# Expert passes of a decoder step: a ring of eleven up slabs, and TensorE's up products written out

## The chip, the cores and the metric

The kernel runs on one core of a Trainium2 chip. The metric is the device time of one execution in microseconds (us). TensorE is called PE here, VectorE DVE, ScalarE ACT and SyncE SP, as in the profile. SP issues nearly all transfers (DMAs); PE's own instructions are fetched by the DMA engines too, and the profile counts them as "instruction" packets.

## The reference

Two layers of a decoder trunk on 288 tokens (256 of a prompt, 8 x 4 of samples), model width 1024. Each layer has a token mixer (three recurrent branches, gates, an output projection) and a feed-forward part. In layer 0 that is dense, in layer 1 it is a mixture of eight experts, two for each token. All is fp32.

```python
def moe_swiglu(h, router, w1, w3, w2):          # w1, w3: 8 x 1024 x 2816, w2: 8 x 2816 x 1024
    logits = (h @ router).astype(jnp.float32)
    top_v, top_i = lax.top_k(logits, TOP_K)
    probs = jax.nn.softmax(top_v, axis=-1)
    gate = jnp.sum(jax.nn.one_hot(top_i, N_EXPERTS) * probs[..., None], axis=-2)
    out = jnp.zeros(h.shape, jnp.float32)
    for e in range(N_EXPERTS):
        out = out + gate[..., e:e + 1] * ((silu(h @ w1[e]) * (h @ w3[e])) @ w2[e])
    return out
```

## The kernel before

The whole step is one program. The change bears on its last part, `experts`, and on one place of `mix_out` just before it.

**Passes.** Each expert is one pass over its own tokens, gathered into at most 91, 88, 73, 85, 76, 82, 79 and 70 columns in the eight passes (`CAPS`). Seven passes are written out one behind the other for PE and SP (`FIXED`), each with its own width; the eighth stands in a loop that runs `rest` times (once in the profiled execution) to take in an overflow.

**Slabs.** Weights come in slabs of 128 partitions x 8 blocks x 128 columns, 512 KB. A pass has 44 up slabs (22 pairs of w1 and w3, `UP_SLABS`) and 24 down slabs (`DOWN_SLABS`; 8 of them hold 384 KB). Up slabs go through `ring`, eight places that the rest of the program uses too; slab n lies in place n % 8. Down slabs go through six places in the dead tensor `proj` (`DRING`). Each landing adds 16 to the place's semaphore (`slab_in`, `down_in`), each slab that PE has finished adds 1 to `slab_done`, and a load waits on that count.

**SP's order in a pass** (L2519 to L2541), all in one queue, each load waiting for its own place: down slabs 0 to 5 of this pass; up slabs 8 to 43; the number of the following expert; that expert's up slabs 4 to 7 and 0 to 3 (`FREED`); down slabs 6 to 23. The last pass loads eight up slabs of a following expert, too, which nobody reads.

**PE's order in a pass** (`expert`, L2681): the up products, 44 slabs, as a loop of five turns over eight slabs (`Fori`, body of 8 calls of `up`) and then four slabs behind the loop, 12 slabs of code. A slab is 16 matmuls, K block by K block, each in two halves of 64 output rows (`narrow_products`, L454). The trace has two matmul records and two weight loads for each of them, so 32 and 32 a slab. Then the scatter matrix (L2648), the gathering of the next pass's tokens (L2619, L2626), and a loop of four turns over the 24 down slabs (L2661), the scatter of the results into `xT` (L2672) and transposes (L2679).

Products of pair f go to the PSUM banks 2f % 4 and 2f % 4 + 1; ACT takes silu of the first (L2744), DVE multiplies (L2958), and counts `w1_free` and `w3_free` hold PE back until a bank is free. Inside the loop the values waited for are worked out from its turn in registers.

**Before the experts.** In `mix_out` of layer 1, SP loads the second group of the gate and branch slabs (`load_group`), the eight slabs of the output projection (`load_first_group`), and then up slabs 0 to 7 of expert 1. The tensors `y_ret` and `lora_w` hold sums of activations and weights for the first three pairs of slabs of the join and nothing after that.

Of the kernel before, what the change touches and what calls it, by code (L numbers as in the profile page):

```python
# [20 lines left out]
ACT = mybir.ActivationFunctionType  # L21

D = 1024
# [64 lines left out]


UP_SLABS = 2 * FT  # L90
DOWN_SLABS = 24
HALF = T // 2
PAIRS_UP, PAIRS_DOWN = KT // 2, FT // 2
# [127 lines left out]
def build(nc, xT_in, w_mix, w_lora, w_rank, w_gkup, vec_in, vecf_in, router_in, w_ff, s_ret, s_gla, s_rw,  # L221
# [130 lines left out]
            self.end = w.at  # L352

    slab_in = [nc.alloc_semaphore(name=f"slab_in{s}") for s in range(RING)]
    slab_done = nc.alloc_semaphore(name="slab_done")
    rank_in = [nc.alloc_semaphore(name=f"rank_in{s}") for s in range(2)]
    wr = lora_w[:, :, :].rearrange("p k n -> p (k n)")[:, 0:512].rearrange("p (s n) -> p s n", s=2)
# [77 lines left out]
    def slab_arrived(pe, p, g, s):  # L435
        pe.wait_ge(slab_in[s], (g + (fills_before(layer, s) + fills(p, s) + 1)) * 16)

    def load_ff_slab(sp, e, j, s, done, n=KT):

        sp.wait_ge(slab_done, done)  # L440
        sp.dma_start(ring[:, s, 0:n], w_ff[e, j, :, 0:n]).then_inc(slab_in[s], 16)
# [5 lines left out]
            mm = nc.tensor.matmul(out, ring[:, s, k, :], x, start=(k0 + k == 0), stop=(k0 + k == last - 1))  # L447
        mm.then_inc(slab_done, 1)

    def narrow_products(pe, s, out, rhs, n=KT, k0=0, last=KT):  # L450

        for k in range(n):
            for c in range(2):
                mm = nc.tensor.matmul(out[64 * c:64 * c + 64], ring[:, s, k, 64 * c:64 * c + 64], rhs[:, k0 + k, :],  # L454
                                      start=(k0 + k == 0), stop=(k0 + k == last - 1))
        mm.then_inc(slab_done, 1)

    FIRST, MIDDLE, LAST_TWO = bank[0:6:3], bank[1:6:3], bank[2:6:3]
# [1665 lines left out]
    def mix_out(nc, block, sig, layer, delta, joined):  # L2124
# [31 lines left out]
        @block.sync  # L2156
        def _(sp):
            load_group(sp, S_RW_OUT, 1)
            load_first_group(sp, S_OUT)
            if dense:  # L2160
                for j in range(FF_SLABS):
                    load_ff_slab(sp, 0, j, j % RING, FF0 + j - RING + 1, dense_slab_width(j))
                    if j == UP_SLABS:
                        sp.wait_ge(sig("normed"), KT)
                        sp.dma_start(vec[:, :], vec_in[layer + 1]).then_inc(sig("next_vec"), 16)
                        sp.dma_start(lora_w[:, :, :], w_lora[layer + 1]).then_inc(sig("next_low"), 16)
                        sp.dma_start(gkup[:, :], w_gkup[layer + 1]).then_inc(sig("next_up"), 16)
                load_next_layer(sp)
                sp.wait_ge(sig("next_up"), 16)
            else:  # L2170
                for j in range(RING):
                    load_ff_slab(sp, 1, j, j, FF0 + j - RING + 1)
# [287 lines left out]
    def experts(nc, block, sig, layer, merge, rs):  # L2460
# [26 lines left out]
        down_in = [sig(f"down_in{s}") for s in range(DRING)]  # L2487
        LG, LT, RANK = bank[6], bank[1], bank[0][:, 0:4 * NE]
        HG, SC, DOWN, SUM = bank[4:8], bank[1], bank[2:4], bank[0]
        OTOK, ADD = (bank[6], bank[4]), (bank[7], bank[5])  # L2490
        FF0 = slabs_before(layer, len(STREAM))
        FREED = 4, 5, 6, 7, 0, 1, 2, 3
        TILES = ((0, 128), (128, 128), (256, 32))

        def passes(eng):
# [3 lines left out]
        def count(p, per, k):  # L2499

            i, done = p
            return i * per + (done * per + k)
# [5 lines left out]
        @block.sync  # L2508
        def _(sp):
            def freed_up(p, n):  # L2510

                if n >= RING:
                    return count(p, FF_SLABS, FF0 + n - RING + 1)
                return count(p, FF_SLABS, FF0 - FF_SLABS + max(range(n, UP_SLABS, RING)) + 1)

            def load_up(p, e, n):
                load_ff_slab(sp, e, n, n % RING, freed_up(p, n))

            def load_down(p, e, d):  # L2519
                if d >= DRING:  # L2520
                    sp.wait_ge(slab_done, count(p, FF_SLABS, FF0 + UP_SLABS + d - DRING + 1))
                else:
                    sp.wait_ge(slab_done, count(p, FF_SLABS, FF0 - DRING + d + 1))
                n = slab_width(UP_SLABS + d)
                sp.dma_start(down_ring[:, d % DRING, 0:n], w_ff[e, UP_SLABS + d, :, 0:n]).then_inc(down_in[d % DRING], 16)

            e = 1
            for q in range(FIXED):
                p = 0, q
                for d in range(DRING):  # L2530
                    load_down(p, e, d)
                for n in range(RING, UP_SLABS):
                    load_up(p, e, n)
                if q == 0:
                    sp.wait_ge(sig("ctl"), 1)
                following = sp.value_load(ctl[0:1, q:q + 1], min_val=1, max_val=NE)
                for n in FREED:
                    load_up((0, q + 1), following, n)
                for d in range(DRING, DOWN_SLABS):
                    load_down(p, e, d)  # L2540
                e = following  # L2541
            rest = passes(sp)
            with sp.Fori(0, rest) as i:
                e = sp.value_load(ctl[0:1, bass.ds(i + (FIXED - 1), 1)], min_val=1, max_val=NE)
                following = sp.value_load(ctl[0:1, bass.ds(i + FIXED, 1)], min_val=1, max_val=NE)
                p = i, FIXED
                for d in range(DRING):
                    load_down(p, e, d)
                for n in range(RING, UP_SLABS):
                    load_up(p, e, n)  # L2550
                for n in FREED:
                    sp.wait_ge(slab_done, freed_up((i, FIXED + 1), n))
                    settle(sp)
                    sp.dma_start(ring[:, n], w_ff[following, n]).then_inc(slab_in[n], 16)
                for d in range(DRING, DOWN_SLABS):
                    load_down(p, e, d)
            for k in range(0, KT, 2):
                sp.wait_ge(sig("normed"), k + 2)
                sp.dma_start(yT_out[:, k:k + 2, :], hT[:, k:k + 2, :]).then_inc(sig("stored"), 16)
            sp.wait_ge(sig("stored"), 4 * 16)  # L2560
            for s in range(RING):
                per = len(range(s, UP_SLABS, RING))
                fill = fills_before(layer, s) + fills(len(STREAM), s) + FIXED * per + 1
                sp.wait_ge(slab_in[s], rest * (per * 16) + fill * 16)
                settle(sp)

        @block.tensor
        def _(pe):
# [44 lines left out]
            def gather_tokens(n, cap):  # L2613

                pe.wait_ge(sig("picked"), n)
                for j in range(2):
                    for r in range(4):
                        rows = slice(NS * r, NS * r + NS)
                        mm(HG[r][:, CAP * j:CAP * j + cap], htok2[rows, j, :], gather[rows, 2, 0:cap], start=(j == 0),  # L2619
                           stop=False)  # L2620
                for r in range(4):
                    for j in range(2):
                        k = 4 * j + r
                        for i in range(2):
# [3 lines left out]
                                          start=False, stop=(j == 1 and i == 1))  # L2628
                    last.then_inc(sig("hg_ps"), 1)

            def up(p, cap, n, turn):

                i, done = p
                s = n % RING
                per = len(range(s, UP_SLABS, RING))
                fill = fills_before(layer, s) + fills(len(STREAM), s) + done * per + n // RING + 1
                pe.wait_ge(slab_in[s], turn * 16 + (i * (per * 16) + fill * 16))
                pe.wait_ge(sig("w3_free" if n % 2 else "w1_free"), turn * (RING // 2) + count(p, FT, n // 2 + 1))
                if n in (2, 3):
                    pe.wait_ge(sig("oT"), count(p, KT, n - 1))  # L2640
                narrow_products(pe, s, bank[n % 4][:, 0:cap], hg[:, :, 0:cap])

            def scatter_matrix(p):

# [36 lines left out]
            def expert(p, cap, next_cap):  # L2681

                pe.wait_ge(sig("hg"), count(p, 1, 1))
                settle(pe)
                with pe.Fori(0, UP_SLABS // RING) as g:
                    for n in range(RING):
                        up(p, cap, n, g)
                for n in range(UP_SLABS // RING * RING, UP_SLABS):
                    up(p, cap, n, 0)
                scatter_matrix(p)  # L2690
                pe.wait_ge(sig("otok"), count(p, KT, 2))
                pe.wait_ge(sig("added"), count(p, KT, 2))
                gather_tokens(count(p, 1, 2), next_cap)
                pe.wait_ge(sig("w3_free"), count(p, FT, FT + 2))
                settle(pe)
                with pe.Fori(0, KT // 2) as t:
                    for m in range(2):
# [38 lines left out]
        def _(act):  # L2736
            ac, cp = nc.scalar.activation, ACT.Copy

            def silu(p, f):
                act.wait_ge(slab_done, count(p, FF_SLABS, FF0 + 2 * f + 1))  # L2740
                if f == 0:
                    settle(act)
                act.wait_ge(sig("w3_free"), count(p, FT, f + 1))
                ac(act1[:, f % 2, :], bank[2 * f % 4][:, 0:CAP], ACT.Silu).then_inc(sig("w1_free"), 1)  # L2744

            def take_down(p, m):
                act.wait_ge(slab_done, count(p, FF_SLABS, FF0 + UP_SLABS + 3 * m + 3))
# [58 lines left out]
        def _(dve):  # L2806
# [144 lines left out]
            def expert(p):  # L2951

                for f in range(FT):
                    dve.wait_ge(slab_done, count(p, FF_SLABS, FF0 + 2 * f + 2))
                    if f == 0:
                        settle(dve)
                    dve.wait_ge(sig("w1_free"), count(p, FT, f + 3))
                    tt(hid[:, f, :], bank[(2 * f + 1) % 4][:, 0:CAP], act1[:, f % 2, :],  # L2958
                       ALU.mult).then_inc(sig("w3_free"), 1)
                    choose(p, f)  # L2960
                take_gathered(count(p, 4, 4))
# [348 lines left out]
```

## Time and profile before

| | us |
|---|---|
| median of 3 runs | 2516.02 |
| lowest and highest run | 2513.42, 2517.08 |
| the profiled execution's own time | 2513.11 |
| its span in the trace | 2511.3 |
| expert passes in the trace, first up product to last transpose | 1770.8 to 2497 |

The page gives for each engine its busy time, and the load in 40 equal slices of the span (62.8 us each): the last twelve slices are the expert passes. A line of the timeline is a run of instructions of one kind: start, length, engine and line, shapes, count, and in brackets the idle time before it with what ended it. "Issue" there means that the engine waited for nothing that the profile shows as a semaphore or a transfer. A line of the busy times by stretch gives start and end, length, and each engine's busy time in it with its count, the granted clock (1.00 is 2.4 GHz), the share of the DMA engines and what they moved.

### The profile page before, as it was taken

To read this page: it belongs to the slowest core of one execution; us is meant where nothing else is said; L and a number is where in the kernel's file an instruction comes from. 1 tells how busy PE (TensorE), PEld (TensorE's weight loads), DVE (VectorE), ACT (ScalarE), POOL (GpSimd) and SP (SyncE) were. 2 spreads that over 40 slices of the span, in tenths; PEclk is the share of its full clock that TensorE was granted. 3 is DMA by queue.
4 is the path that set the end of the run, shared out by engine and by line. 5 is a ranking of instruction groups with operands and counts; after the bars stand their busy time and mean duration, and the time that the engine had idled before them with its cause. 6 is when DMAs were issued, how large, how long until landed. Compare 5 with 4: busy or idle time off the path is not lost. (4 is left out here: it accounts for less than half of the span.)

```text
span 2511.3 us, 103490 instructions
## 1 busy us (share of the span) xinstructions
PE 2442.6 (97%) x45930; PEld 2040.3 (81%) x45930; DVE 1291.6 (51%) x3328; ACT 609.9 (24%) x1798; POOL 0.2 (0%) x4
## 2 busy tenths in 40 slices
PE   9999999999999999999999999999999999999997
PEld 7987666666699999998766666678999899888986
DVE  7666666666686676756576666667311111111111
ACT  2233333433311101233333334421111111111111
POOL 0000000000000000000000000000000000000000
PEclk9999999999999999999999999999999999999999
DMA  6334442222243454333353222234899999999997
GB/s 248 111 136 161 151 133 88 83 83 79 99 154 136 153 173 144 128 124 139 129 168 129 84 78 77 83 112 154 341 342 390 393 392 370 402 372 374 402 388 274
DMA packets 146091, 500.85 MB, mean 199 GB/s; under 512 B 18784, under 2 KB 23520, under 8 KB 143360
## 3 DMA queue, kind: packets, MB, share of 16 engines
q1 hardware_dynamic: 145792, 496.44, 54.7%
q8 instruction: 239, 3.92, 0.6%
q14 instruction: 60, 0.49, 0.1%
HBM read 476.08 MB, written 20.29 MB: 198 GB/s over the span
## 5 line engine op out<-in xcount | busy, mean ns | idle before, releaser
L301 PE MATMUL psum<-hT,ring 128*64 128x144 f32 (+1 forms) x4568 | 457.4, 346 | 3.7 <-DVE hT L2421 1.7
L454 PE MATMUL psum<-work,ring 128*64 128x91 f32 (+7 forms) x11264 | 422.0, 234 | 15.7 <-issue 7.3
L454 PEld LDWEIGHTS psum<-work,ring 128*64 128x64 f32 x11264 | 404.7, 136 | 33.3 <-issue 23.8
L301 PEld LDWEIGHTS psum<-hT,ring 128*64 128x64 f32 x4568 | 293.3, 137 | 96.2 <-issue 12.1
L2958 DVE TENSOR_TENSOR work<-psum,work 128x91 f32<-128x91 f32 x176 | 44.6, 253 | 365.4 <-PE psum L454 365.2
L2661 PE MATMUL psum<-work,proj 128*64 128x91 f32 (+7 forms) x5632 | 208.9, 234 | 10.6 <-issue 9.2
L2661 PEld LDWEIGHTS psum<-work,proj 128*64 128x64 f32 x5632 | 202.3, 137 | 16.1 <-issue 10.3
L1767 ACT ACTIVATE work<-psum 128x256 f32<-128x256 f32 (+4 forms) x320 | 104.1, 362 | 349.7 <-PE psum L1678 84.8
L301 PE MATMUL psum<-work 128*64 128x144 f32 (+4 forms) x2096 | 154.1, 282 | 4.3 <-DVE work L1258 3.6
L301 PE MATMUL psum<-y_ret,work 128*64 128x144 f32 x2400 | 156.3, 286 | 0.5 <-DVE y_ret L531 0.5
L301 PEld LDWEIGHTS psum<-y_ret,work 128*64 128x64 f32 x2400 | 148.7, 137 | 0.9 <-issue 0.9
L2949 DVE TENSOR_TENSOR xT<-xT,psum 128x288 f32<-128x288 f32 x64 | 29.1, 455 | 228.6 <-PE psum L2672 227.6
L301 PEld LDWEIGHTS psum<-work 128*64 128x64 f32 (+2 forms) x2096 | 121.3, 136 | 30.6 <-issue 11.3
L2744 ACT ACTIVATE work<-psum 128x91 f32<-128x91 f32 x176 | 43.5, 247 | 377.5 <-PE psum L454 377.5
L301 PE MATMUL psum<-y_ret,ring 128*64 128x144 f32 (+1 forms) x1280 | 126.8, 332 | 2.5 <-ACT work L1767 2.5
L301 PEld LDWEIGHTS psum<-y_ret,ring 128*64 128x64 f32 x1280 | 79.5, 137 | 18.4 <-ACT work L1767 4.5
L323 PE MATMUL psum<-hT,ring 128*128 128x288 f32 x252 | 72.8, 408 | 0.0
L2748 ACT ACTIVATE work<-psum 128x91 f32<-128x91 f32 x64 | 15.9, 248 | 228.1 <-PE psum L2661 228.1
L1563 PEld LDWEIGHTS psum<-work 64*64 64x64 f32 x1408 | 47.3, 134 | 29.4 <-issue 17.7
L546 DVE TENSOR_TENSOR y_gla<-psum,y_gla 128x288 f32<-128x288 f32 x72 | 33.0, 458 | 72.8 <-PE psum L301 72.2
L301 PE MATMUL psum<-hT,work 128*64 128x144 f32 x928 | 68.8, 287 | 0.0
L518 DVE TENSOR_TENSOR work<-ring 128x512 f32<-128x512 f32 (+1 forms) x90 | 54.7, 608 | 19.0 <-PE psum L301 19.0
(513 smaller groups left out, 3733.5 us busy)
## 6 DMA issues: line engine op xcount, KB each, us to landing
ring<-w_ff_dram SPq DMA_DIRECT2D x424, 512.0 KB, 7.3
ring<-w_mix_dram SPq DMA_DIRECT2D x256, 512.0 KB, 4.1
proj<-w_ff_dram SPq DMA_DIRECT2D x128, 512.0 KB, 5.3
proj<-w_ff_dram SPq DMA_DIRECT2D x64, 384.0 KB, 5.6
work<-s_gla_dram SPq DMA_DIRECT2D x8, 1024.0 KB, 5.3
gla_s_out<-work SPq DMA_DIRECT2D x8, 1024.0 KB, 4.7
work<-s_ret_dram SPq DMA_DIRECT2D x8, 512.0 KB, 5.4
ret_s_out<-work SPq DMA_DIRECT2D x8, 512.0 KB, 3.0
```

Of the source, the lines that this page charges most:

```text
L301: last = nc.tensor.matmul(out[64 * c:64 * c + 64], weights[:, 64 * c:64 * c + 64], x, start=start, stop=stop)
L323: mm = (in_halves if self.narrow else nc.tensor.matmul)(out, ring[:, s, k, :], rhs[:, k, :], start=(k == 0), stop=(k == KT - 1))
L454: mm = nc.tensor.matmul(out[64 * c:64 * c + 64], ring[:, s, k, 64 * c:64 * c + 64], rhs[:, k0 + k, :], start=(k0 + k == 0), stop=(k0 + k = ...
L518: op.tensor_tensor(s1, a21, a22, ALU.add).then_inc(sig("wsum"), 1)
L546: nc.vector.tensor_tensor(c[:, 1:3, :], two(LAST_TWO[side]), c[:, 5:7, :], ALU.add).then_inc(sig("outer"), 1)
L1563: last = mm(unit(half(W, r), c), half(AT, 1 - r)[:, c], half(X, 1 - r)[:, c], start=True, stop=True)
L1767: return nc.scalar.activation(out, in_, func, **kw)
L2661: last = mm(DOWN[m][64 * h:64 * h + 64, 0:cap], down_ring[:, d, k, 64 * h:64 * h + 64], hid[:, KT * c + k, 0:cap], start=(KT * c + k == 0) ...
L2744: ac(act1[:, f % 2, :], bank[2 * f % 4][:, 0:CAP], ACT.Silu).then_inc(sig("w1_free"), 1)
L2748: ac(oT[:, m % 2, :], DOWN[m % 2][:, 0:CAP], cp).then_inc(sig("oT"), 1)
L2949: tt(xT[:, k, :], xT[:, k, :], ADD[m % 2][:, 0:T], ALU.add).then_inc(sig("added"), 1)
L2958: tt(hid[:, f, :], bank[(2 * f + 1) % 4][:, 0:CAP], act1[:, f % 2, :], ALU.mult).then_inc(sig("w3_free"), 1)
```

## The change

Three slabs more are kept for the up products. The new places 8, 9 and 10 lie in `y_ret` (two) and `lora_w` (one), with semaphores of their own (`extra_in`); up slab n lies in place n % 11, and 44 is four times eleven. The load order of a pass becomes: down slabs 0 to 5; up slabs 11 to 43; the following expert's slabs 0 to 10; down slabs 6 to 23. Slabs 8 to 10 of the first expert are loaded in `mix_out`, ahead of the slabs of the output projection, as soon as pair 2 of the join is done.

PE's loop over the up slabs goes: 44 calls of `up` stand one behind the other in each of the eight passes, with constants for what they wait for in the seven fixed ones. The PSUM banks of each pair are the same as before. In the gathering of tokens the matmuls of the samples are regrouped, two banks at a time; their number stays.

```diff
+UP_RING = 11
+    extra_in = [nc.alloc_semaphore(name=f"extra_in{s}") for s in range(UP_RING - RING)]
+    up_in = slab_in + extra_in
+    extra_slots = [x.rearrange("p k n -> p (k n)")[:, D * j:D * j + D].rearrange("p (k n) -> p k n", k=KT)
+                   for x, j in ((y_ret[:, :, :], 0), (y_ret[:, :, :], 1), (lora_w[:, :, :], 0))]
+    up_slots = [ring[:, s] for s in range(RING)] + extra_slots
+    def up_fills(s):
+        return fills_before(layer, s) + fills(len(STREAM), s) if s < RING else 0
...
             load_group(sp, S_RW_OUT, 1)
+            if not dense:
+                sp.wait_ge(slab_done, join_done(BRANCH0 - 1))
+                for n in range(RING, UP_RING):
+                    sp.dma_start(up_slots[n], w_ff[1, n]).then_inc(up_in[n], 16)
             load_first_group(sp, S_OUT)
...
-                if n >= RING:
-                    return count(p, FF_SLABS, FF0 + n - RING + 1)
-                return count(p, FF_SLABS, FF0 - FF_SLABS + max(range(n, UP_SLABS, RING)) + 1)
+                if n >= UP_RING:
+                    return count(p, FF_SLABS, FF0 + n - UP_RING + 1)
+                return count(p, FF_SLABS, FF0 - FF_SLABS + UP_SLABS - UP_RING + n + 1)
...
-                for n in range(RING, UP_SLABS):
+                for n in range(UP_RING, UP_SLABS):
                     load_up(p, e, n)
...
-                for n in FREED:
+                for n in range(UP_RING):
                     load_up((0, q + 1), following, n)
...
-            def up(p, cap, n, turn):
+            def up(p, cap, n):
...
-                pe.wait_ge(slab_in[s], turn * 16 + (i * (per * 16) + fill * 16))
-                pe.wait_ge(sig("w3_free" if n % 2 else "w1_free"), turn * (RING // 2) + count(p, FT, n // 2 + 1))
+                pe.wait_ge(up_in[s], i * (per * 16) + fill * 16)
+                pe.wait_ge(sig("w3_free" if n % 2 else "w1_free"), count(p, FT, f + 1))
...
-                with pe.Fori(0, UP_SLABS // RING) as g:
-                    for n in range(RING):
-                        up(p, cap, n, g)
-                for n in range(UP_SLABS // RING * RING, UP_SLABS):
-                    up(p, cap, n, 0)
+                for n in range(UP_SLABS):
+                    up(p, cap, n)
                 scatter_matrix(p)
```

## Rows read from the trace of the kernel before

**Rows 1.** The page: busy times, GB/s in 40 slices, instruction packets.
```profile
span 2511.3 us, 103490 instructions
PE 2442.6 (97%) x45930; PEld 2040.3 (81%) x45930; DVE 1291.6 (51%) x3328; ACT 609.9 (24%) x1798; POOL 0.2 (0%) x4
...
GB/s 248 111 136 161 151 133 88 83 83 79 99 154 136 153 173 144 128 124 139 129 168 129 84 78 77 83 112 154 341 342 390 393 392 370 402 372 374 402 388 274
...
q8 instruction: 239, 3.92, 0.6%
```

**Rows 2.** Busy times by stretch: up products of passes 3 and 6, sum of eight.
```profile
1956.60:2009.80 53.20, 50.91 (x1410) 47.14 (x1409) 8.65 (x29) 8.03 (x26) 0.00 (x0) 1.00 1.02 406
...
2223.90:2280.90 57.00, 52.27 (x1410) 51.00 (x1409) 8.58 (x29) 8.40 (x26) 0.00 (x0) 1.00 1.01 388
...
sum 437.00, PE 421.72 PEld 404.86 DVE 72.59 ACT 62.30 POOL 0.00; mean PE 52.72 PEld 50.61 DVE 9.07 ACT 7.79 POOL 0.00
```

**Rows 3.** Busy times by stretch: sum of the eight stretches behind the up products.
```profile
sum 289.15, PE 276.58 PEld 248.32 DVE 41.09 ACT 32.69 POOL 0.00; mean PE 34.57 PEld 31.04 DVE 5.14 ACT 4.09 POOL 0.00
```

**Rows 4.** Timeline of PE: up products of pass 1, and some of pass 3.
```profile
1770.80 55.95 PE L454 MATMUL psum<-work,ring 128*64 128x91 f32 x1408 [0.20 <-issue]
...
1976.79 10.00 PE L454 MATMUL psum<-work,ring 128*64 128x73 f32 x256 [0.24 <-DMA ring<-w_ff_dram]
1987.03 10.00 PE L454 MATMUL psum<-work,ring 128*64 128x73 f32 x256 [0.24 <-DMA ring<-w_ff_dram]
```

**Rows 5.** Waits of PE, 1770 to 2497: us in total, times, longest.
```profile
PE psum L2661 <- issue: 9.2, 8, 2.3
PE psum L454 <- issue: 7.3, 12, 1.7
PE psum L454 <- DMA ring<-w_ff_dram: 5.2, 18, 1.5
```

**Rows 6.** Timeline of PE: first up products of pass 2 and pass 6.
```profile
1870.31 4.99 PE L454 MATMUL psum<-work,ring 128*64 128x88 f32 x125 [0.31 <-issue]
1875.82 44.58 PE L454 MATMUL psum<-work,ring 128*64 128x88 f32 x1160 [0.52 <-issue]
...
2230.20 4.72 PE L454 MATMUL psum<-work,ring 128*64 128x82 f32 x126 [1.43 <-issue]
2236.62 41.50 PE L454 MATMUL psum<-work,ring 128*64 128x82 f32 x1120 [1.70 <-issue]
```

**Rows 7.** DMA queues (packets, MB, share), 1873.5:1873.7, 2466.6:2466.8, 2288.1:2288.3, 2236.6:2274, 2274:2290, 1690:1700.
```profile
q8 instruction: 1, 0.02, 30.0%
...
q8 instruction: 1, 0.02, 31.6%
...
q8 instruction: 1, 0.02, 32.2%
...
q1 hardware_dynamic: 3998, 14.59, 100.8%
...
q8 instruction: 3, 0.05, 1.3%
...
q8 instruction: 2, 0.03, 1.4%
```

**Rows 8.** Busy times of PE, clock, DMA share, GB/s, from one block's entry on.
```profile
1870.31:1875.82 5.51, 4.99 (x125) 1.00 0.95 333
2100.51:2107.13 6.62, 4.69 (x126) 1.00 1.00 378
2230.20:2236.62 6.42, 4.72 (x126) 1.00 0.97 349
2462.74:2469.19 6.45, 4.13 (x124) 0.98 0.99 365
...
2107.13:2111.45 4.32, 4.32 (x88) 1.00 0.82 283
...
2286.28:2290.55 4.27, 4.26 (x120) 1.00 0.95 334
```

More of the change, by code:

```diff
@@ L448, in slab_products, with narrow_products @@
         mm.then_inc(slab_done, 1)
[L450 to L455, printed above, removed]
+    def narrow_products(out, slab, rhs):
+        for k in range(KT):
+            mm = in_halves(out, slab[:, k, :], rhs[:, k, :], k == 0, k == KT - 1)
         mm.then_inc(slab_done, 1)
@@ L2489, in experts @@
         HG, SC, DOWN, SUM = bank[4:8], bank[1], bank[2:4], bank[0]
+        UP_BANK = [bank[2 * (f % 2):2 * (f % 2) + 2] for f in range(FT)]
         OTOK, ADD = (bank[6], bank[4]), (bank[7], bank[5])
         FF0 = slabs_before(layer, len(STREAM))
-        FREED = 4, 5, 6, 7, 0, 1, 2, 3
         TILES = ((0, 128), (128, 128), (256, 32))
@@ L2510, in freed_up @@
             def freed_up(p, n):
-                if n >= RING:
-                    return count(p, FF_SLABS, FF0 + n - RING + 1)
-                return count(p, FF_SLABS, FF0 - FF_SLABS + max(range(n, UP_SLABS, RING)) + 1)
+                if n >= UP_RING:
+                    return count(p, FF_SLABS, FF0 + n - UP_RING + 1)
+                return count(p, FF_SLABS, FF0 - FF_SLABS + UP_SLABS - UP_RING + n + 1)
             def load_up(p, e, n):
-                load_ff_slab(sp, e, n, n % RING, freed_up(p, n))
+                sp.wait_ge(slab_done, freed_up(p, n))
+                sp.dma_start(up_slots[n % UP_RING], w_ff[e, n]).then_inc(up_in[n % UP_RING], 16)
             def load_down(p, e, d):
@@ L2548, in _ @@
                     load_down(p, e, d)
-                for n in range(RING, UP_SLABS):
+                for n in range(UP_RING, UP_SLABS):
                     load_up(p, e, n)
-                for n in FREED:
+                for n in range(UP_RING):
                     sp.wait_ge(slab_done, freed_up((i, FIXED + 1), n))
                     settle(sp)
-                    sp.dma_start(ring[:, n], w_ff[following, n]).then_inc(slab_in[n], 16)
+                    sp.dma_start(up_slots[n], w_ff[following, n]).then_inc(up_in[n], 16)
                 for d in range(DRING, DOWN_SLABS):
@@ L2560, in _ @@
             sp.wait_ge(sig("stored"), 4 * 16)
[L2561 to L2564, printed above, removed]
+            for s in range(UP_RING):
+                per = UP_SLABS // UP_RING
+                sp.wait_ge(up_in[s], rest * (per * 16) + (up_fills(s) + FIXED * per + 1) * 16)
                 settle(sp)
@@ L2615, in gather_tokens @@
                 pe.wait_ge(sig("picked"), n)
[L2616 to L2620, printed above, removed]
-                for r in range(4):
+                for r in range(4):
+                    if r % 2 == 0:
+                        for j in range(2):
+                            for q in range(r, r + 2):
+                                rows = slice(NS * q, NS * q + NS)
+                                mm(HG[q][:, CAP * j:CAP * j + cap], htok2[rows, j, :], gather[rows, 2, 0:cap],
+                                   start=(j == 0), stop=False)
                     for j in range(2):
@@ L2629, in gather_tokens @@
                     last.then_inc(sig("hg_ps"), 1)
-            def up(p, cap, n, turn):
+            def up(p, cap, n):
                 i, done = p
-                s = n % RING
-                per = len(range(s, UP_SLABS, RING))
-                fill = fills_before(layer, s) + fills(len(STREAM), s) + done * per + n // RING + 1
-                pe.wait_ge(slab_in[s], turn * 16 + (i * (per * 16) + fill * 16))
-                pe.wait_ge(sig("w3_free" if n % 2 else "w1_free"), turn * (RING // 2) + count(p, FT, n // 2 + 1))
+                s, f = n % UP_RING, n // 2
+                per = UP_SLABS // UP_RING
+                fill = up_fills(s) + done * per + n // UP_RING + 1
+                pe.wait_ge(up_in[s], i * (per * 16) + fill * 16)
+                pe.wait_ge(sig("w3_free" if n % 2 else "w1_free"), count(p, FT, f + 1))
                 if n in (2, 3):
                     pe.wait_ge(sig("oT"), count(p, KT, n - 1))
-                narrow_products(pe, s, bank[n % 4][:, 0:cap], hg[:, :, 0:cap])
+                narrow_products(UP_BANK[f][n % 2][:, 0:cap], up_slots[s], hg[:, :, 0:cap])
             def scatter_matrix(p):
@@ L2743, in silu @@
                 act.wait_ge(sig("w3_free"), count(p, FT, f + 1))
-                ac(act1[:, f % 2, :], bank[2 * f % 4][:, 0:CAP], ACT.Silu).then_inc(sig("w1_free"), 1)
+                ac(act1[:, f % 2, :], UP_BANK[f][0][:, 0:CAP], ACT.Silu).then_inc(sig("w1_free"), 1)
             def take_down(p, m):
@@ L2957, in expert @@
                     dve.wait_ge(sig("w1_free"), count(p, FT, f + 3))
-                    tt(hid[:, f, :], bank[(2 * f + 1) % 4][:, 0:CAP], act1[:, f % 2, :],
+                    tt(hid[:, f, :], UP_BANK[f][1][:, 0:CAP], act1[:, f % 2, :],
                        ALU.mult).then_inc(sig("w3_free"), 1)
```

## The prediction

> **What bounds the kernel now.** I read the page first. TensorE is busy 97% of the span, and in the last twelve slices the DMA moves 341 to 402 GB/s (274 in the very last) where it moved 77 to 173 in most slices before [rows 1]. So only the expert passes, 1770.8 to 2497, bear on this change, and there two resources are nearly full at once. Then I asked for the busy times by stretch: the eight stretches in which PE does its 44 up slabs take 437.0 us together, 54.6 each [rows 2], and the eight behind them (last gathers, 24 down slabs, add-ups) 289.15 us, 36.1 each [rows 3].
>
> Two paces can set the up stretches. With 91 columns PE does its 1408 recorded matmuls (32 a slab) in 55.95 us without a break, 1.27 us a slab. With 73 columns the transfers set it: 256 matmuls, eight slabs, start every 10.24 us (1976.79, 1987.03), each time after a wait for the ring [rows 4]. That is 0.524 MB in 1.28 us, 410 GB/s, which I take as the DMA's limit. The whole pass is 66 slabs' worth of bytes (44 + 16 + 8 x 0.75), 84.5 us at that pace, against an actual 90.8 (726 / 8). So the DMA idles some 6 us a pass, because the ring is full in the down stretch, and PE is starved some microseconds in the up stretch: this is what a deeper ring aims at.
>
> The third limit is easily overlooked, PE's own instructions. The waits show "issue" as large as the transfers: 7.3 us ahead of the up products and 9.2 ahead of the down products, against 5.2 for the ring [rows 5]. The timeline tells where. In the second pass the up products pause at 1870.31 and again at 1875.82, 125 matmuls later. In the sixth they pause until 2230.20 and, 126 matmuls later, until 2236.62 [rows 6]. 125 matmuls with their weight loads and some register work are 256 instructions, and the page has 239 instruction packets of 3.92 MB, 16 KB each, 64 bytes an instruction [rows 1]. So the pauses are at the ends of fetched blocks. One packet lies between the two pauses of the second pass; it starts at about 1873.6, 3.3 us after PE has entered the block before and 2.2 us ahead of PE's restart. In the last pass a packet starts at about 2466.7, in a block that PE enters at 2462.74, and PE restarts at 2469.19 [rows 7, 8]. The reading: **the next block is asked for when PE enters the present one**, one ahead and no more, and lands 4 to 6.6 us later. A block lasts PE 3.9 us (70 columns) to 5.0 us (91). Once the up loop's body of eight slabs is in, it runs without a single such packet: from 2236.6 to 2274 the queues show none of PE's [rows 7]. That is why the pauses are confined to the first turn of each loop and to the code behind it.
>
> **The change part by part.**
>
> *Up products written out.* Before, a pass holds 8 + 4 up slabs of code, now 44. That is 32 slabs more, 64 instructions each, 2048: eight blocks more a pass, 64 in all. An up stretch is 44 x 64 / 252 = 11.2 blocks, each of which has to arrive under the load of its own weight stream. The price of a block is the later of PE's own time (4.45 us on average over the widths) and the fetch. For the fetch [rows 8] has both sides, block entry to readiness: 5.51 us at 333 GB/s, 6.62 at 378, 6.42 at 349 and 6.45 at 365, where PE was caught; and some 4.3 at 283 to 334, where it was not (there the windows run from the entry to the packet's start plus 2.35 us; the packet of the second is at 2288.2 [rows 7]). A written-out stretch at a period P moves 3.94 slabs, 2.07 MB, in P: 376 GB/s at 5.5 us, 344 at 6.0. It regulates itself between the two sorts of row. Half and half of 6.25 and 4.3, with PE's own 4.45 as the floor, is 5.35; the first blocks of a stretch still share the DMA with the last down slabs. I take **5.5 us**. Up stretch: 11.2 x 5.5 = 61.6 us. Against 54.6: +7.0 a pass, **+56 us** for eight. Ends: 4.9 (little above PE's own time) gives 54.9, +2 us in all; 6.25, the mean of the four caught ones, gives 70.0, +123 us.
>
> On this the Trainium skill speaks for the change. "Runtime: NRT & Kernel Launch", section "Instruction fetch mechanics", says that the sequencer fetches the next page while executing the current one, that the crossing is mostly hidden, and that kernels prefer full unrolling since branches break the prefetch. The one-ahead fetch agrees with the trace; "mostly hidden" does not: in the block of 6.62 us PE is busy for 4.69. By the page this part would cost nothing, by the rows 56 us.
>
> *Loop removed.* The branches and the register arithmetic of the waits go: no idle time is seen at the loop's turns in pass 1 [rows 4], so I cost it at 0 (bounds: -0.3 us a turn, the smallest pause that the timeline names beside it, and 0). The pauses of the first turn, 7.3 us in all, don't go: they are part of the 11.2 blocks.
>
> *Ring of eleven.* Three slabs more can wait in memory: at most 3 x 1.28 = 3.84 us of DMA time that a pass can bring forward. Worth that only where PE waits for the ring. With PE at 5.5 / 3.94 = 1.40 us a slab and the DMA at 1.28 nobody waits for the ring any more, so in my sum the ring brings **0**; at the other end it brings 6 x 3.84 = 23 us, in the six passes with under 88 columns.
>
> *Next expert's slabs.* Eleven instead of eight stand in the SP queue ahead of down slabs 6 to 23; the order 0 to 10 instead of 4 to 7, 0 to 3 follows the new slots. Each is issued when a slab of the last eleven is done, at PE's pace, so at the end of the up stretch about one is under way and down slab 6 is late by nothing. Cover gone (DMA-bound up stretch): up to 3.84 us a pass. The last pass loads three slabs more that nobody reads, 3.84 us of DMA, hidden by the same argument; bounds 0 to 3.84 us.
>
> *Early loads.* Three slabs of expert 1 go ahead of the output projection's eight loads on SP's queue, waiting for pair 2 of the join. Those eight wait for pair 3 and later anyway, and the DMA moves under 160 GB/s just before [rows 1]: 0, at most 3.84 us once. The regrouped gather keeps its instruction count: 0, either way under its own 0.7 us.
>
> Sum: 2513.1 (profiled execution, span 2511.3) + 56 = 2569. The median of the runs lies 2.9 us higher: **2572 us**.
>
> **The rivals.**
>
> *The fetch keeps ahead in straight code.* What I see might be a loop's after-effect: after a backward branch the fetcher restarts one block behind, and in long straight code it gets ahead. For it: straight code before 1760 needs two packets in 10 us and isn't stopped by them. Against it: it draws about half the bandwidth there, so one ahead is enough; and behind the loop's exit, where the code is straight for three blocks, the three packets are spread over 16 us and each is followed by a pause or nearly so [rows 7]. Then the ring's 23 us come in, and some 2 us of pauses: 2516 - 25 = **2491 us**, faster. It decides if blocks are ready in under 4 us. The Trainium skill's section on instruction fetch, named above, comes to this.
>
> *The fetch gets quick once the queue drains.* As in the rows of 4.3 us: period 4.9, +2 us, with some of the early stretch slower: 2513 to 2532, **2522 us**.
>
> *The fetch stays slow.* 6.25 us a block, +123: **2639 us**. Against: at that period the load is 330 GB/s, where two rows of three (333, 334, 283) are quick.
>
> *The ring starves the down slabs.* Only where the up stretch is DMA-bound, 3.84 us a pass; it would cancel the gain of the first rival (2514), small, and counted there.
>
> **How the numbers follow.** Forecast, a fetch-bound up stretch with 5.2 to 5.9 us a block (2545 to 2608): 0.62. Fetch hidden: 0.16. Quick fetch: 0.13. Slow fetch: 0.09. About 5 us (0.2%) can be told from no change. Faster: 0.16 and a little of the quick case, 0.17. Same: half of the quick case, 0.06. Slower: 0.77. The range 2500 to 2615 leaves out most of the hidden case (0.11) and most of the slow one (0.07).
>
> **What would show it.** PE's instruction packets 239 -> about 303. Up stretches of 60 to 64 us whatever the width, where they ran from 53.2 to 57; pauses put down to "issue" every 125 or 126 matmuls through a whole up stretch, 0.5 to 2 us each, and no wait for the ring. DMA at 360 to 390 GB/s there. Stretches behind the ups unchanged within 1 us each. The down stretch shows that the argument holds where the loop stayed. Wrong if pauses are absent after the first two blocks of a pass, or if two instruction packets come within 3 us of each other.

## The result, and the profile after

The changed kernel takes 2579.18 us (median of 4 runs, 2576.36 to 2579.69) against 2515.12 for the kernel before, run beside it: ratio 1.0255, 95% interval 1.0241 to 1.0268. The forecast was 2572, slower. The profiled execution has a span of 2577.0 us, 65.7 more than before.

The page of the changed kernel: the span, TensorE, the load in 40 slices, PE's instruction packets, and two groups of matmuls of 64 output rows, those that read `ring` (nearly all of them up products) and those that read `y_ret`. L302 is the helper that now issues the up products, L2675 the down products.

```profile
span 2577.0 us, 103269 instructions
...
PE 2452.2 (95%) x45930; PEld 2053.0 (80%) x45930; DVE 1290.6 (50%) x3328; ACT 609.2 (24%) x1798; POOL 0.2 (0%) x4
...
GB/s 242 109 133 164 164 122 82 80 83 81 119 139 149 152 177 121 157 109 145 142 157 90 81 77 75 96 180 261 332 361 337 342 364 342 347 379 350 344 368 261
...
q8 instruction: 304, 4.98, 0.8%
...
L302 PE MATMUL psum<-work,ring 128*64 128x88 f32 (+8 forms) x8800 | 363.4, 241 | 47.6 <-issue 47.5
...
L302 PE MATMUL psum<-work,y_ret 128*64 128x91 f32 (+7 forms) x2048 | 85.1, 238 | 16.2 <-issue 16.2
```

As many matmuls and about as many instructions as before, 65 instruction packets more (304 against 239, [rows 1]), and the DMA at 332 to 379 GB/s in its last twelve slices (261 in the very last) where it was at 341 to 402 (274). The chip moves nearly the same bytes more slowly, because something else holds PE. The waits of PE in the expert passes (us in total, times, longest) name it:

```profile
PE psum L302 <- issue: 73.5, 62, 2.7
PE psum L2675 <- issue: 2.9, 3, 1.4
PE psum L2675 <- DMA proj<-w_ff_dram: 2.1, 4, 0.8
```

Before, "issue" held the up products 7.3 us in 12 places, and the ring 5.2 us in 18 [rows 5]. Now it is 73.5 us in 62 places, and the wait for the ring is gone altogether. The busy times by stretch (start and end, length, PE's busy time and count, granted clock, DMA share, GB/s), the up products of passes 1, 3 and 6 and the sum of all eight, then the sum of the eight stretches behind them:

```profile
1770.80:1832.10 61.30, 57.52 (x1409) 1.00 0.94 352
...
1972.50:2036.50 64.00, 52.71 (x1409) 0.90 0.97 364
...
2269.00:2329.40 60.40, 53.56 (x1409) 0.97 0.99 383
...
sum 498.30, PE 425.28; mean PE 53.16
...
sum 292.90, PE 283.71; mean PE 35.46
```

The up stretches grew from 437.0 to 498.3 us [rows 2], which is 61.3 of the 65.7 us; the stretches behind them from 289.15 to 292.9 [rows 3]. The length of an up stretch no longer follows the width: 60.4 to 64.1 us for 70 to 91 columns. The timeline of the last pass (70 columns) shows how it comes about:

```profile
2464.86 7.43 PE L302 MATMUL psum<-work,ring 128*64 128x70 f32 x234 [0.61 <-issue]
2473.51 0.89 PE L302 MATMUL psum<-work,ring 128*64 128x70 f32 x22 [1.22 <-issue]
...
2479.76 9.51 PE L302 MATMUL psum<-work,ring 128*64 128x70 f32 x248 [2.23 <-issue]
...
2513.90 5.69 PE L302 MATMUL psum<-work,ring 128*64 128x70 f32 x125 [2.50 <-issue]
2519.95 2.48 PE L302 MATMUL psum<-work,ring 128*64 128x70 f32 x74 [0.37 <-issue]
```

Between the pauses at 2473.51 and 2479.76 lie 125 matmuls, between those at 2513.90 and 2519.95 again 125: one fetched block each, PE at work for 4 us of the first and waiting for its successor for 2.2.

### The profile page after: what moved, and what is told of

Same layout as the page of the kernel before. It is cut to its first block and busy times, and to the rows that moved or that the text cites. A ratio compares the mean times of both kernels' runs of the same rounds, so it can differ in the third digit from the quotient of the medians.

```text
span 2577.0 us, 103269 instructions
## 1 busy us (share of the span) xinstructions
PE 2452.2 (95%) x45930; PEld 2053.0 (80%) x45930; DVE 1290.6 (50%) x3328; ACT 609.2 (24%) x1798; POOL 0.2 (0%) x4
## 5 line engine op out<-in xcount | busy, mean ns | idle before, releaser
L302 PE MATMUL psum<-hT,ring 128*64 128x144 f32 (+1 forms) x4568 | 457.0, 345 | 4.4 <-DVE hT L2434 1.7
L302 PE MATMUL psum<-work,ring 128*64 128x88 f32 (+8 forms) x8800 | 363.4, 241 | 47.6 <-issue 47.5
L302 PEld LDWEIGHTS psum<-work,ring 128*64 128x64 f32 x8800 | 344.5, 140 | 55.6 <-issue 54.5
L302 PEld LDWEIGHTS psum<-hT,ring 128*64 128x64 f32 x4568 | 291.7, 137 | 98.3 <-issue 12.7
L2675 PE MATMUL psum<-work,proj 128*64 128x91 f32 (+7 forms) x5632 | 207.6, 233 | 5.7 <-issue 2.9
L2675 PEld LDWEIGHTS psum<-work,proj 128*64 128x64 f32 x5632 | 200.8, 136 | 11.6 <-issue 4.2
L302 PE MATMUL psum<-work 128*64 128x144 f32 (+4 forms) x2096 | 154.9, 282 | 4.3 <-DVE work L1267 3.6
L302 PE MATMUL psum<-y_ret,work 128*64 128x144 f32 x2400 | 156.2, 286 | 1.2 <-DVE y_ret L540 1.2
L302 PEld LDWEIGHTS psum<-y_ret,work 128*64 128x64 f32 x2400 | 148.7, 137 | 1.5 <-issue 1.5
L302 PEld LDWEIGHTS psum<-work 128*64 128x64 f32 (+2 forms) x2096 | 122.0, 136 | 30.6 <-issue 11.4
L302 PE MATMUL psum<-y_ret,ring 128*64 128x144 f32 (+1 forms) x1280 | 127.2, 332 | 2.5 <-ACT work L1776 2.5
L302 PE MATMUL psum<-work,y_ret 128*64 128x91 f32 (+7 forms) x2048 | 85.1, 238 | 16.2 <-issue 16.2
L302 PEld LDWEIGHTS psum<-y_ret,ring 128*64 128x64 f32 x1280 | 79.9, 137 | 18.4 <-ACT work L1776 4.5
L302 PEld LDWEIGHTS psum<-work,y_ret 128*64 128x64 f32 x2048 | 80.1, 141 | 18.0 <-issue 17.9
```

What stands on the lines that cost most here:

```text
L302: last = nc.tensor.matmul(out[64 * c:64 * c + 64], weights[:, 64 * c:64 * c + 64], x, start=start, stop=stop)
L2675: last = mm(DOWN[m][64 * h:64 * h + 64, 0:cap], down_ring[:, d, k, 64 * h:64 * h + 64], hid[:, KT * c + k, 0:cap], start=(KT * c + k == 0) ...
```

## The experiments

**Which part of the change costs.** The written-out code alone, in the kernel before:

```diff
-                with pe.Fori(0, UP_SLABS // RING) as g:
-                    for n in range(RING):
-                        up(p, cap, n, g)
-                for n in range(UP_SLABS // RING * RING, UP_SLABS):
-                    up(p, cap, n, 0)
+                for n in range(UP_SLABS):
+                    up(p, cap, n, 0)
```

> The kernel before with one edit: PE's 44 up slabs of each pass written out, ring of eight kept. Theory (the instruction fetch under load sets the pace): as slow as the changed kernel, 2570 to 2590 us, 303 to 305 instruction packets of PE, up stretches of 60 to 64 us, and the ring of eight starves nobody at that pace. Rival (the deeper ring, its places or its load order cost the time, three slabs of the next expert ahead of the down slabs): within 8 us of the kernel before, 2508 to 2524. Rival (both share the loss): 2535 to 2560.

Measured: 2578.46 us, ratio 1.0247 (1.0230 to 1.0265) to the kernel before. Its page has 304 packets as well, its up stretches sum to 497.6 us, and PE waits 80.1 us for instructions at the up products:

```profile
PE psum L454 <- issue: 80.1, 63, 2.8
PE psum L2661 <- issue: 6.6, 6, 2.6
```

So the written-out code carries the whole loss. The rest of the change together (ring of eleven, load order, early loads, regrouped gather) makes no difference that the runs can tell: 1.0247 and 1.0255, with intervals that overlap.

**Is it the load that makes the fetch late?** Each up slab is loaded only in part; the rest of it isn't loaded, and PE multiplies what lies there. The kernel before and the changed one, both with half:

```diff
-                sp.dma_start(up_slots[n % UP_RING], w_ff[e, n]).then_inc(up_in[n % UP_RING], 16)
+                sp.dma_start(up_slots[n % UP_RING][:, 0:KT // 2], w_ff[e, n, :, 0:KT // 2]).then_inc(
+                    up_in[n % UP_RING], 16)
```

> The kernel before, each up slab of the expert passes loaded only in half (blocks 0 to 3 of 8; PE multiplies what else lies there), so that the DMA moves about 220 GB/s in the up stretches. PE's own pace is left: 44 slabs at 0.99 to 1.27 us, 49.9 us a stretch on average, 35 to 45 us less than before: 2470 to 2482 us. It is the yardstick for the same cut in the changed kernel.

> The changed kernel with the same cut, each up slab loaded only in half, blocks 0 to 3. Theory (a block is late because its packet queues behind the weight stream): at half the load a block is ready in 3.5 to 4.5 us, under PE's 3.9 to 5.0, so the pauses go and it is within 10 us of the other cut kernel, 2470 to 2490 us. Rival (each of the 64 blocks more costs about 1 us by itself, whatever the load): 55 to 65 us above the other cut kernel, 2525 to 2545 us.

Measured: 2462.54 us and 2487.73 us, one run each. The packets are 239 and 304 as ever. Busy times by stretch of the changed kernel with half slabs, passes 2 (88 columns), 3 (73) and 8 (70), and the sum; then the sum of the other kernel with half slabs:

```profile
1869.10:1922.70 53.60, 53.60 (x1409) 1.00 0.73 236
...
1959.40:2009.50 50.10, 46.49 (x1409) 1.00 0.76 250
...
2389.50:2437.90 48.40, 45.26 (x1408) 1.00 0.76 250
...
sum 412.40, PE 401.84; mean PE 50.23
```

```profile
sum 398.70, PE 396.52; mean PE 49.57
```

The first is 8 us under what was expected. Between the two I had expected 10 us at the most; it is 25. Of these, 13.7 lie in the up stretches, where the full load had made 61.3, 6.8 in the stretches behind (284.0 against 277.2), and 4.4 before the first pass. The pass of 88 columns has no pause at all; those of 73 and 70 columns idle 3 to 4 us a stretch. Nine blocks have a pause at either end, at 190 to 245 GB/s, and last 4.3 to 5.2 us, median 4.7. PE needs 4.0 us for a block with 73 columns (44.8 us for a stretch of 11.2 blocks in the other kernel with half slabs) and 4.8 with 88.

The two traces also show where the time of a fetch goes. In the changed kernel the packet of the next block starts 3.5 us (median) after PE has entered the present one, with half slabs 2.3 us; from the packet's start to PE's restart it is 2.4 us in both. The load lengthens what comes before the packet starts. To see whether that is a floor, the same with an eighth of each slab:

```diff
+                sp.dma_start(up_slots[n % UP_RING][:, 0:1], w_ff[e, n, :, 0:1]).then_inc(
```

> The changed kernel, each up slab of the expert passes loaded only in its first of 8 blocks (PE multiplies what else lies there): the DMA moves some 60 GB/s in the up stretches. With half the slab (236 to 250 GB/s) the widths of 91 and 88 columns had no pause and that of 73 had blocks of 4.5 us, 0.4 over PE's own time. Theory (the load makes the fetch late): at 60 GB/s a block is ready in under 3.9 us, no pause at any width, up stretches at 44 to 56 us, 400 in sum, 2460 to 2472 us. Rival (a fetch takes 4.4 us at the least): the pauses of the narrow passes stay, up stretches 412 in sum.

Measured: 2472.52 us, one run, at the upper end of what was expected. The waits of PE at the up products, and the stretches of passes 3 and 8 with the sum:

```profile
PE psum L302 <- issue: 1.1, 2, 0.7
```

```profile
1960.40:2005.50 45.10, 45.04 (x1410) 1.00 0.32 98
...
2377.50:2421.70 44.20, 44.03 (x1408) 1.00 0.32 98
...
sum 396.70, PE 395.88; mean PE 49.49
```

With the same 304 packets and the same straight code the pauses are down from 73.5 us to 1.1. There is no floor of 4.4 us. What a block costs is set by the load of the weight stream, which delays the start of its packet. Not all of the distance is pauses, though: this kernel is still 10 us behind the kernel before with half slabs, 5.5 before the first up product (1776.1 against 1770.6) and 6.2 in the stretches behind (283.4 against 277.2), with the up stretches 2 us shorter. No run says what these are.

**Is it the count of instructions?** The changed kernel with each pair of half-width matmuls as one:

```diff
-            mm = in_halves(out, slab[:, k, :], rhs[:, k, :], k == 0, k == KT - 1)
+            mm = nc.tensor.matmul(out, slab[:, k, :], rhs[:, k, :], start=(k == 0), stop=(k == KT - 1))
```

> The changed kernel with each up product as one matmul of 128 output rows and not two of 64: 8 matmuls a slab, 32 recorded instructions and not 64, the same arithmetic. 32 x 44 = 1408 instructions are 5.6 blocks a stretch, a block lasts eight slabs, at least 8 us, far over the 5.6 us of a fetch. Theory: 304 - 8 x 5.5 = about 260 packets, no pauses for instructions in the up stretches, which then run at PE's own pace for whole matmuls, not known at 91 columns: the projection's whole matmuls with 288 columns take 0.58 us each, scaled to 91 columns 1.46 us a slab and to 70 columns 1.12, with 1.28 us of the DMA as the floor, 56 to 62 us a stretch. 2510 to 2570 us. Rival (the written-out code is slow for another reason than the count of its instructions, its waits with constants or its places in y_ret and lora_w): pauses stay, 2575 or more.

Measured: 2701.72 us. The two sides of the expectation come apart. The pauses went (0.6 us left) and the packets are 260, as said; PE's own pace was far off:

```profile
1771.50:1850.10 78.60, 78.60 (x704) 1.00 0.85 281
...
2569.30:2647.98 78.68, 78.65 (x704) 1.00 0.86 298
```

78.6 us for 704 recorded matmuls, 112 ns each, with 91 columns as with 70. At this pace the weights load the DMA with only 281 to 298 GB/s, so count and load changed together here; a block of 256 instructions lasts PE some 14 us, far more than any fetch in these traces. A whole matmul doesn't get shorter with its columns here. It is two records, 223 ns, where the two halves that it replaces are four records of 40 ns with 91 columns (55.95 us for 1408, [rows 4]), 159 ns. Scaling from 288 columns was no price for this.

**How much code is held, and what a block costs in between.** The kernel before with a body of sixteen slabs, two turns and twelve slabs behind:

```diff
+                with pe.Fori(0, 2) as g:
+                    for n in range(16):
+                        up(p, cap, n, g)
+                for n in range(32, UP_SLABS):
+                    up(p, cap, n, 0)
```

> The kernel before with a loop body of sixteen up slabs, two turns, and twelve slabs behind. 1024 instructions are 4.1 blocks. If PE holds them, the second turn runs without packets: 239 + 8 x 4 = 271 packets and about half of the changed kernel's loss, since 28 of 44 slabs are straight or first-turn code, not 12: 16 slabs more are 4 blocks a pass, 32 in all, of about 1 us: 2535 to 2550 us. If it doesn't, the second turn fetches again, 300 packets or more and 2565 to 2590 us, with a wait at the turn.

Measured: 2542.09 us, ratio 1.0114 (1.0097 to 1.0131), and 272 packets: 1024 instructions are held over a turn, and 33 blocks more cost 28 us, 0.85 us a block. The other loop, over the down slabs, written out in the kernel before:

```diff
-                with pe.Fori(0, KT // 2) as t:
+                for t in range(KT // 2):
```

> The kernel before with the other loop written out: PE's four turns over the down slabs, the up loop kept. A turn is 352 recorded instructions for the down products and some 20 of other kinds, so three turns more of code are about 1120 instructions, 4.4 blocks a pass, 35 in all: about 274 packets. PE's own time for a block is longer here, since the scatter products with 288 columns lie among them: a turn of 6.9 to 8.5 us is 1.46 blocks, 4.7 to 5.8 us a block, 5.2 on average. Theory (a block costs what its fetch, some 5.0 to 5.6 us at this load, exceeds PE's own time): 0.2 to 0.6 us for each of the 35 blocks, 7 to 21 us: 2520 to 2534 us. Rival (each block of straight code costs 1 us as in the up stretches): 2548 or more. Rival (a turn of the loop costs as much as it saves): 2511 to 2517.

Measured: 2532.03 us, ratio 1.0076 (1.0062 to 1.0090), 274 packets, and 22.3 us of waits in place of 9.2:

```profile
PE psum L2661 <- issue: 22.3, 24, 1.8
```

35 blocks more, 20 us, 0.57 us a block: the upper end of what was expected, and 0.4 us less than a block costs in the up stretches (64 us for 65 blocks), where PE has less to do in each.

**What is the deeper ring worth where a loop is kept?** Eleven places don't allow a loop, since 11 slabs are 5.5 pairs and the banks would change roles; twelve do.

```diff
-UP_RING = 11
+UP_RING = 12
+                with pe.Fori(0, UP_SLABS // UP_RING) as g:
+                    for n in range(UP_RING):
+                        up(p, cap, n, g)
+                for n in range(UP_SLABS // UP_RING * UP_RING, UP_SLABS):
+                    up(p, cap, n, 0)
```

> The changed kernel with a ring of twelve (the twelfth place in lora_w, too) and the loop put back: three turns over twelve slabs and eight slabs behind. Theory: a body of 12 x 64 = 768 instructions, some 3.1 blocks, is still held by PE, about 247 packets; the ring's depth then counts: four slabs more, up to 5.1 us in each of the six passes with under 88 columns, 2485 to 2508 us, faster than both kernels. If PE doesn't hold four or five blocks, each turn fetches its body again: 300 packets and 2560 to 2590 us. Rival (the ring is what costs): slower than the kernel before although there is a loop, 2525 or more.

Measured: 2516.36 us beside 2513.17, ratio 1.0012 (1.0002 to 1.0022), 256 packets. A miss: the loop gives the 63 us back, but the ring brings nothing. The sum of the up stretches, the stretches behind passes 5 and 8, and the sum of those behind:

```profile
sum 420.10, PE 402.28; mean PE 50.28
...
2187.80:2227.60 39.80, 37.58 (x832) 0.91 0.99 372
...
2457.80:2496.30 38.50, 36.21 (x834) 0.91 0.91 356
sum 305.20, PE 290.10; mean PE 36.26
```

The up stretches are 17 us shorter than before, and the stretches behind them 16 us longer. I took this for the twelve loads that stand ahead of down slab 6, and moved four of them behind down slabs:

```diff
+        ORDER = [(0, n) for n in FREED[:8]]
+        for j in range(4):
+            ORDER += [(1, DRING + 3 * j + c) for c in range(3)] + [(0, FREED[8 + j])]
+        ORDER += [(1, d) for d in range(DRING + 12, DOWN_SLABS)]
```

> The ring of twelve with the loop, and another order on SP's queue: eight of the next expert's slabs, then down slabs 6, 7, 8, one up slab, down 9, 10, 11, one up slab and so on, so that four up slabs less stand ahead of the down slabs. In the run without this the up stretches were 15.4 us shorter in sum (420.2 against 435.6) and the stretches behind them 14.4 us longer (304.4 against 290.0). Theory (the twelve slabs ahead of down slab 6 take back what the ring gives): stretches behind at 290 to 296, up stretches at 418 to 424, 2498 to 2508 us. Rival (the longer stretches behind come from later instruction blocks, two more of them a pass, and not from the order): no change, 2512 to 2520.

Measured: 2527.23 us, slower still, ratio 1.0057 (1.0040 to 1.0074). The theory fell (the stretches behind sum to 320.1 us, not 290 to 296), and the rival of no change with it. Three turns over the down slabs in pass 3:

```profile
2016.45:2023.54 7.09, 7.09 (x190) 1.00 0.83 265
2023.54:2033.22 9.68, 7.78 (x187) 1.00 1.01 404
2033.22:2042.86 9.64, 7.77 (x187) 1.00 1.03 409
```

SP issues no load from 2006.4 to 2017.9 (in the run without this edit from 2008.7 to 2014.3). By its order the next load is down slab 6, whose place comes free only when PE has finished down slab 0, while four up slabs stand behind it. The DMA runs out of work and moves 265 GB/s in the first turn; afterwards too much is left, and PE waits 19.9 us for `proj` in the eight passes, against 0.8 in the run without this edit. Here the next expert's slabs are better loaded while the down places are all taken. In the run without this edit PE's waits were the following:

```profile
PE psum L302 <- issue: 18.4, 18, 2.6
PE psum L2677 <- issue: 7.2, 7, 2.1
PE psum L2642 <- issue: 3.3, 4, 1.4
PE psum L2636 <- issue: 1.4, 1, 1.4
```

30.3 us for instructions, against 17.9 before (7.3 + 9.2 + 1.4, the last in the gathering). The code is 20 slabs long a pass, not 12, which is 16 blocks more in the eight passes. But 11.1 of these 12 us lie at the up products (18.4 against 7.3), in stretches that are shorter all the same: they take from what the ring gives there. The 16 us behind are something else, mostly PE's own work. The matmuls that gather the next tokens are busy 12.5 us (samples, L2636) and 25.2 us (prompt, L2642), against 5.9 and 19.6 before. Some 5 to 6 of these 12 us belong to the regrouped order, and much of the rest to passes 5 and 8: there the granted clock is 0.61 and 0.50 in the 5 us behind a pause of 1.4 us (2190 to 2195 and 2460.9 to 2466), and the gather takes 6.6 and 6.0 us where the other passes take 3.9 to 4.6. Longer waits for instructions are 1.3 us of the 16; the last 2 to 3 us stay open.

**The regrouped gather.** It was costed at nothing. In the trace of the kernel before with the new order its small matmuls take 1.41 us a pass where they took 0.74, 5.4 us in eight passes. Alone in the kernel before, taken out of the ring of twelve, and taken out of the changed kernel:

```diff
-                for j in range(2):
-                    for r in range(4):
...
+                    if r % 2 == 0:
+                        for j in range(2):
+                            for q in range(r, r + 2):
```

> The kernel before with only the regrouped gather of the changed kernel (matmuls of the samples in two groups of four, each ahead of two banks). In the changed kernel a group of 8 recorded matmuls takes 0.66 us, and in the kernel before all 16 take as much, because four row groups are at work at once there and two here. Theory: 0.75 us more in each of eight passes between the up and the down products, 6 us: 2517 to 2522 us beside 2513 to 2515. Rival (my prediction's 0: a wait behind it takes the 0.75 us up): within 2 us of the kernel before.

> The ring of twelve with the loop (2516 us) and the old order of the gather. Theory: 6 us less than with the regrouped one, 2507 to 2512 us, and with that the first kernel of the study that is faster than the kernel before, by 2 to 7 us. Up stretches 418 to 424 us in sum. Rival: 2515 to 2518, nothing gained.

> The changed kernel with the old order of the gather. Theory: 6 us less, 2570 to 2575 us. Rival (the pauses for instructions shift and take it up): 2577 to 2582.

Measured: 2514.05 us (ratio 1.0005, 0.9996 to 1.0014); 2519.15 us (1.0028, 1.0016 to 1.0040); 2573.86 us (1.0257, 1.0240 to 1.0273, an interval that holds the changed kernel's 1.0255). The first says that it costs between -1 and 3.5 us, not 6, which is the rival's case; the second that the ring of twelve gains nothing by taking it out, and is slower than the kernel before; the third lies where it was expected, but can't be told from the changed kernel. In the second run the pauses for instructions grew to 40.2 us (20.0 + 14.1 + 4.4 + 1.7). The trace of the first has the longer matmuls in each pass and 1.9 us less pauses in the down products, 7.3 for 9.2: it looks as if a gather that ends earlier only makes PE wait longer for the block behind it, which no run tried by itself. No version that loads all of the weights beats the kernel before.

## Why the prediction was right

*The bound.* It rested on a third limit, read from a few pauses at the heads of loops. That held: 304 packets where about 303 were forecast, 62 pauses, none of them for the ring.

*One block ahead.* In the up stretches of the changed kernel there are 44 blocks of 120 to 128 matmuls with a pause at either end. Each has exactly one instruction packet in it, and the packet starts 2.4 us (median) before PE restarts. That the packet is asked for just when PE enters a block stays a reading; the traces show when it starts, not when it was asked for. The rival "the fetch keeps ahead in straight code" fell.

With it fell, for this kernel, two sentences of the Trainium skill, "Runtime: NRT & Kernel Launch", section "Instruction fetch mechanics": that the crossing of a block is "mostly hidden", and that kernels prefer full unrolling. PE idles 73.5 us at the crossings, and the two loops written out cost 2.5% and 0.8%. The Trainium skill's one-block lookahead agrees with the one packet in each block, and with an eighth of the load the crossing is hidden indeed (1.1 us of pauses).

*The price of a block.* 5.5 us was taken, 44 slabs in 11.2 blocks; measured is 498.3 / 8 / 11.2 = 5.56. The up stretches were forecast at +56 us and came to +61.3; 0.06 us a block in 90 blocks is the difference. The way to the 5.5 was less good than the number. I let the fetch get quicker as the load falls from 380 to 340 GB/s. The 44 caught blocks, in thirds by load (two left over), average 5.87 us at 345 GB/s, 5.75 at 373 and 5.89 at 400: flat. The mean comes down only by the blocks that were not caught, and the fetch gets quicker somewhere between 340 and 250 GB/s (4.7 us, half slabs). The "slow fetch" rival, 6.25 us, was therefore nearer than its price of 123 us looks, and that the half-and-half of 6.25 and 4.3, rounded up, came so close was in part luck.

*The stretches behind.* Forecast unchanged within 1 us each; three of the eight are not (+2.4, +2.6 and -2.0 us), and the sum is +3.75. The regrouped gather alone doesn't explain it: with the written-out code and the old gather the sum is 294.5, 5.4 more than before.

*The loop's branches, 0.* Not told apart: every run that takes the loop away adds blocks too.

*The ring, 0.* Right in the sum: the ring of eight with the same code takes the same time, and no wait for the ring is left in the changed kernel. What I named as its other end, 23 us if nobody waits for instructions, wasn't reached with a ring of twelve and the loop either: 17 us came in the up stretches and 16 went behind them. The rival "the ring starves the down slabs" did not show: there PE waits 0.8 us for `proj`, before 1.0, and with fewer loads ahead of the down slabs it got worse.

*Early loads, 0.* Open. The first up product starts at 1770.8 in the changed kernel as before. In the eight traces with the early loads it starts between 1770.8 and 1776.1, mean 1773.0, in the six without between 1769.8 and 1771.9, mean 1770.8. No run took them alone.

## What to carry to other kernels

Where a stream of weights fills the DMA, PE's instructions are part of the traffic: count 256 instructions for each block and compare PE's time for them with what a fetch takes under that load. If PE is the quicker, keep the loop as long as its further turns need no packets: here its removal cost 63 us. A longer straight tail eats part of what a deeper ring gives. Before a ring is made deeper, look whether its size still allows the loop.

## What I had not expected

**The clock falls at some of the pauses.** In the changed kernel the expert passes have ten pauses of over 2 us (2.05 to 2.72), in passes 3 to 6 and 8, and the granted clock falls at each of them and at no shorter one; this is the 0.90 of pass 3 above. Length alone doesn't decide it. With the written-out code and the ring of eight it falls at six of fourteen such pauses, and with the ring of twelve and the loop it falls behind two of 1.4 us. The last pass of the changed kernel, a block that ends in a pause and the stretches right behind two of them:

```profile
2473.51:2479.76 6.25, 4.02 (x125) 1.00 1.03 416
2479.76:2484.00 4.24, 4.24 (x93) 0.65 1.03 411
...
2513.90:2519.60 5.70, 5.69 (x125) 0.70 1.01 372
```

0.65 and 0.70 are means over a part at 1.2 GHz and a part at 2.4. The 125 matmuls that take 4.02 us at full clock take 5.69. It seems to cost little here: PE would have waited for the next block anyway, and the pause behind it is only 0.37 us. In the gathers of the ring of twelve, above, it did cost.

**A whole matmul with 128 output rows takes 223 ns with 70 as with 91 columns**, and the two halves of 64 rows that do the same take 159 ns with 91 columns and 126 with 70 (44.2 us for 1408 records, an eighth of the load).

**PE holds a loop body of 1024 instructions** over its turn without fetching it again (272 packets).

**Packets add up.** 239, 256, 272, 274 and 304 packets are the kernel before with 0, 2, 4, 4.4 and 8 blocks more in each of eight passes, to within one packet.
